# Hybrid encoder trunk: another order for the first projection of each layer's head, and thirteen idle transposes left out

## The reference

```python
h = layer_norm(x, ln_in_g, ln_in_b)
for l in range(DEPTH):                       # DEPTH = 2
    proj = h @ w_in[l]                       # 1024 x 2048
    ...                                      # four head groups: windowed attention, gated conv, Fourier mixing, rotary attention
    mix = jnp.concatenate([rms_norm(o, g_i) for each group], axis=-1)
    h = layer_norm(DN_ALPHA * h + mix @ w_out[l], ln1_g[l], ln1_b[l])
    ffn = jnp.square(jax.nn.relu(h @ w1[l])) @ w2[l]
    h = layer_norm(DN_ALPHA * h + ffn, ln2_g[l], ln2_b[l])
return h
```

## Time and profile before

| | |
|---|---|
| median of 3 runs | 1072.41 us (1072.38 to 1072.66) |
| profiled execution | 1072.76 us |
| its span, first to last instruction | 1071.1 us |
| PE busy | 1054.8 us, 98% |
| DVE, ACT, POOL busy | 788.7, 516.7, 91.6 us |
| share of PE in the chain that ended last | 91% |
| mean granted TensorE clock | 0.997 |

### The profile page before, as it was taken

How to read it: one execution, slowest core, us unless ns; L and a number is a source line. 1 busy time by engine, 2 the same in 40 slices (tenths; PEclk the granted TensorE clock), 3 DMA queues, 4 the chain that set the end, 5 groups by cost and what they waited for, 6 DMA issues and landing times.

```text
span 1071.1 us, 15587 instructions
## 1 busy us (share of the span) xinstructions
PE 1054.8 (98%) x5310; PEld 896.2 (84%) x5310; DVE 788.7 (74%) x1096; ACT 516.7 (48%) x774; POOL 91.6 (9%) x84
## 2 busy tenths in 40 slices
PE   8999999999999999999999999999999999999996
PEld 6888889998888888888878888899888888888885
DVE  8845886968757758758887568777794784784787
ACT  3433666365355355355624247653643643642651
POOL 5200232100000000000002003221000000000001
PEclk9999999999999999999999999999999999999998
DMA  7432013030521520431233410310234134125122
GB/s 288 158 118 79 1 61 119 2 126 32 205 79 40 181 93 34 166 113 50 109 136 143 157 40 21 118 41 14 114 118 158 40 114 161 39 94 181 39 79 80
DMA packets 17383, 105.54 MB, mean 99 GB/s; under 512 B 2017, under 2 KB 2705, under 8 KB 5793
## 3 DMA queue, kind: packets, MB, share of 16 engines
q1 hardware_dynamic: 15984, 98.70, 25.3%
q0 software_dynamic: 1184, 5.86, 1.7%
q10 hardware_dynamic: 144, 0.07, 0.0%
HBM read 101.49 MB, written 2.10 MB: 97 GB/s over the span
## 4 chain that ended last, share of the span: by engine, by line
PE 91%; issue 4%; DVE 3%; ACT 0%; POOL 0%; DVEq 0%; POOLq 0%
PE bank L449 18%; PE bank L451 18%; PE bank L450 18%; PE bank L753 8%; PE bank L754 8%; PE bank L755 8%; PE bank L699 4%; PE bank L685 2%; PE bank L596 1%; PE bank L597 1%; PE bank L458 1%; PE bank L609 1%; DVE w_raw L1182 0%; PE bank L521 0%; PE bank L522 0%
## 5 line engine op out<-in xcount | busy, mean ns | idle before, releaser
L449 PE MATMUL bank<-h_hi,w_hi 128*128 128x512 f32 (+1 forms) x704 | 260.8, 370 | 0.2
L450 PE MATMUL bank<-h_lo,w_hi 128*128 128x512 f32 (+1 forms) x704 | 260.3, 370 | 0.0
L451 PE MATMUL bank<-h_hi,w_lo 128*128 128x512 f32 (+1 forms) x704 | 260.3, 370 | 0.0
L753 PE MATMUL bank<-w_hi,hid_hi 128*128 128x512 f32 x448 | 174.4, 389 | 0.0
L754 PE MATMUL bank<-w_lo,hid_hi 128*128 128x512 f32 x448 | 174.3, 389 | 0.0
L755 PE MATMUL bank<-w_hi,hid_lo 128*128 128x512 f32 x448 | 174.3, 389 | 0.0
L1163 DVE TENSOR_TENSOR w_lo<-w_raw,w_hi 128x2048 fp32r<-128x2048 f32 x62 | 141.8, 2287 | 36.8 <-ACT w_hi L870 30.0
L449 PEld LDWEIGHTS bank<-h_hi,w_hi 128*128 128x128 f32 x704 | 132.6, 188 | 23.5 <-issue 1.1
L451 PEld LDWEIGHTS bank<-h_hi,w_lo 128*128 128x128 f32 x704 | 132.6, 188 | 22.6
L450 PEld LDWEIGHTS bank<-h_lo,w_hi 128*128 128x128 f32 x704 | 132.6, 188 | 22.3
L870 ACT CAST w_hi<-w_raw 128x2048 fp32r<-128x2048 f32 x56 | 107.1, 1913 | 79.5 <-PE bank L755 56.4
(11 more groups left out here) (174 smaller groups left out, 1638.5 us busy)
## 6 DMA issues: line engine op xcount, KB each, us to landing
w_raw<-in_weights SPq DMA_DIRECT2D x63, 1024.0 KB, 4.8
w_third<-in_weights SPq DMA_DIRECT2D x23, 1024.0 KB, 4.8
rows<-in_rows POOLq DMA_DIRECT2D x4, 1024.0 KB, 5.0
w_raw<-in_weights SPq DMA_DIRECT2D x4, 512.0 KB, 7.3
out_h<-x SPq DMA_DIRECT2D x8, 256.0 KB, 2.0
x<-in_x SPq DMA_DIRECT2D x3, 512.0 KB, 9.6
dft<-in_dft SPq DMA_DIRECT2D x2, 512.0 KB, 7.1
qk_gain<-in_qk_gain POOLq DMA_DIRECT2D x3, 192.0 KB, 3.6
```

Of the source, the lines that this page charges most:

```text
L449: pe.matmul(dst, s_hi, m_hi, start=first, stop=False)
L450: pe.matmul(dst, s_hi, m_lo, start=False, stop=False)
L451: return pe.matmul(dst, s_lo, m_hi, start=False, stop=last)
L753: pe.matmul(bank[dst + t][:], s_hi, m_hi, start=start, stop=False, skip_group_check=goes_on)
```

## The change

Two engines get another order, and thirteen transposes go.

PE: `keep_warm(8)` becomes `keep_warm(1)` and `keep_warm(6)` is left out. In the loop, tile 0 starts with the two products of its own high part with kt 0 and 1, which wait for h_hi only and no longer for h_lo; then the two with its low part, then the two with the low weights of kt 0 and 1; then kt 2 to 7, own high and low in pairs. The turn of tile 1 stands behind all of these. Then come low weights kt 2 and 3 of tile 0, tile 1's eight products of the own high part and its eight of the low part, low weights kt 4 to 7 of tile 0, the turn of tile 2, and the low weights of tile 1. As before, one order serves both layers.

DVE, in layer 1's head alone: the two halves of h_lo of tile 0 now stand between the two halves of tile 1's statistics, and behind its variance.

```diff
-            keep_warm(8)
+            keep_warm(1)
             turn(0, 0)
-            keep_warm(6)
             with pe.Fori(0, DEPTH) as l:
...
-                for t in range(2):
-                    for kt in range(KT):
-                        if t == 0 and kt == 4:
-                            turn(l, 1)
-                        if kt % 4 == 0:
-                            wait(pe, l, "h_lo", 2 * t + kt // 4 + 1)
-                        if t == 0:
-                            high_part_ready(l, kt // PARTS, kt % PARTS)
-                        dst, t_hi, t_lo, m_hi, _ = first_group(t, kt)
-                        pe.matmul(dst, t_hi, m_hi, start=kt == 0, stop=False)
-                        pe.matmul(dst, t_lo, m_hi, start=False, stop=False)
-                for t in range(2):
-                    for kt in range(KT):
-                        if t == 0:
-                            part_ready(l, kt // PARTS, kt % PARTS)
-                        if t == 1 and kt == 0:
-                            turn(l, 2)
-                        dst, t_hi, _, _, m_lo = first_group(t, kt)
-                        last = pe.matmul(dst, t_hi, m_lo, start=False, stop=kt == KT - 1)
-                    last.then_inc(sems["products"], 1)
+                def high_parts(t, kts, own_high):
+                    for kt in kts:
+                        if kt % 4 == 0:
+                            wait(pe, l, "h_hi" if own_high else "h_lo", 2 * t + kt // 4 + 1)
+                        if t == 0 and own_high:
+                            high_part_ready(l, kt // PARTS, kt % PARTS)
+                        dst, t_hi, t_lo, m_hi, _ = first_group(t, kt)
+                        pe.matmul(dst, t_hi if own_high else t_lo, m_hi, start=own_high and kt == 0, stop=False)
+
+                def low_parts(t, kts):
+                    for kt in kts:
+                        if t == 0:
+                            part_ready(l, kt // PARTS, kt % PARTS)
+                        dst, t_hi, _, _, m_lo = first_group(t, kt)
+                        last = pe.matmul(dst, t_hi, m_lo, start=False, stop=kt == KT - 1)
+                    if kt == KT - 1:
+                        last.then_inc(sems["products"], 1)
+
+                first_half, second_half = range(KT // 2), range(KT // 2, KT)
+                for own_high in (True, False):
+                    high_parts(0, range(2), own_high)
+                low_parts(0, range(2))
+                for kt in range(2, KT):
+                    high_parts(0, (kt,), True)
+                    high_parts(0, (kt,), False)
+                turn(l, 1)
+                low_parts(0, range(2, 4))
+                for half in (first_half, second_half):
+                    high_parts(1, half, True)
+                for half in (first_half, second_half):
+                    high_parts(1, half, False)
+                low_parts(0, second_half)
+                turn(l, 2)
+                low_parts(1, range(KT))
                 for t in range(2, TOK):
...
             first_norm(0)
-            input_stats(1)
-            stream_low(0, 0, 0)
+            dve.wait_ge(x_landed[1], 16)
+            row_stats(1, 0)
+            low_half(0, 0, 0, 0)
+            row_stats(1, 1)
+            variance(1, 4, 2, LN_EPS)
+            low_half(0, 0, 0, 1)
             first_norm(1)
```

## The result

| | before | changed |
|---|---|---|
| median, 21 runs each | 1072.85 us (1072.29 to 1074.31) | 1074.31 us (1073.74 to 1075.86) |
| profiled execution | 1072.76 us | 1075.03 us |
| its span | 1071.1 us | 1073.3 us |

The ratio is 1.0014, 95% interval 1.0008 to 1.0020: the changed kernel is slower by 0.9 to 2.1 us of 1073. Forecast were +1.6 us, ratio 1.0015, and a range that holds the measured time; the change is within the 0.2% that the prediction took for the least that can be told from no change. The profiled execution of the change, 2.27 us above that of the kernel before, is one of its slower ones.

The account below looks back on a forecast made before the run. PE's own work was taken to set the time, so order matters only where PE waits, at the two layers' heads. Layer 2 +2.62 and layer 1 -1.03 give +1.6 us, 1074.0 us on the median; range 1073.1 to 1075.1.

Parts of the forecast that it names:

- Layer 2's loss: Layer 2's head: ten more products and a wait delay tile 1's turn; DVE's list carries the whole +2.62 us on.
- the one wait for w_lo part 1: Layer 2's head: PE waits 0.24 us for DVE's part 1 and pays some 0.10 us for a start from idle.
- The further 0.1 for each other wait: Layer 2's head, upper bound +2.8 us: each semaphore wait among the first six products costs a further 0.1.
- Layer 1's start: Layer 1's head: h_hi comes earlier, so PE's first product starts at 10.12 instead of 11.82, -1.70 us.
- Layer 1's gain: Layer 1's head: tile 2's turn at 21.82 instead of 22.85, its products from 24.52 instead of 25.55, -1.03 us.
- a lead of 0.05 was enough: Layer 1's head: DVE, due 0.07 us ahead of POOL, takes the shared port first, as it did in layer 2.
- the first rival: Layer 1's head: POOL has the port before DVE; gain 0.26 instead of 1.03, total +2.36, 1074.8 us; chance 0.24.
- the precedent: Layer 2's head: DVE led POOL's rstd by 0.05 us and had its normal length, while rstd took 1.05 instead of 0.55.
- the forecast order: Layer 1's head: DVE's first centring instruction of tile 2 goes before POOL's part 6 at the shared port.
- The late clock: Layer 1's head: TensorE's clock rises later, tile 0's products run at half speed; total about +3.1, 1075.5 us; chance 0.08.
- The sum: Both heads together: +2.62 - 1.03 = +1.6 us, put on the median as 1074.0 us, +0.15%.

Follow-up runs that it names:

- turn by layer: Changed kernel with tile 1's turn behind eight products in layer 2, as before, and low weights kt 0 and 1 of tile 0 behind that place: 1071.97 us, ratio 0.9989.

## Why the prediction was right

**Layer 2's loss: right, a little small.** Forecast +2.62 us with the bounds 2.3 and 2.8; between the two places lie 528.04 instead of 525.27, +2.77. The mechanism was DVE's list, as said: only its start moved (idle 0.55 to 3.19), its length is 10.02 us as before. Most of the missing 0.15 is in the one wait for w_lo part 1: it cost 0.44 us (0.90 from 537.45 to 538.35, where two products take 0.46) and not 0.34, because DVE began its parts 0.24 us behind PE's first product (536.66 against 536.42) and not 0.14 as in the earlier trace rows. In the second trace, where they began 0.14 behind (537.08 against 536.94), the turn came 4.58 us behind the first product; the forecast makes it 4.55. The further 0.1 for each other wait, which the prediction gave as its upper bound, did not come: the starts behind the first, which takes 0.33 us as before, are 0.23 to 0.24 us apart. Moving the turn alone brings 15.78 of 15.8 forecast, and taking it back for layer 2, together with the two products with low weights, brings the old distance.

**Layer 1's start: right in the first trace.** First half of h_lo 9.91 (10.02 forecast), first product 10.02 (10.12), w_lo part 2 at 12.31 (12.40), tile 1's turn 14.52 (14.56), DVE's centring 17.74 (17.85), part 6 at 17.83 (17.92). The constant 0.1 us is the trace's earlier start of tile 0's norm.

**Layer 1's gain: the step "a lead of 0.05 was enough" failed.** The instant of arrival was forecast within 0.02 us, but the conclusion from it was not safe. In the change's own trace the first rival happened with its numbers: part 7 at 20.80 (20.88), tile 2 at 25.07 (25.19). With DVE first it is 24.30 and 24.43 (24.52). In the row that I took as the precedent, POOL had been idle for 5.28 us before its rstd; here part 6 comes right behind another instruction of its own. That this makes the difference is only argued, and with part 6 behind another instruction both orders occurred. So the chance given to the forecast order rested on a sign that does not decide.

**The late clock** did not come over the products in the change's traces, but was near: the clock rose at 10.01, 10.37, 10.00 and 8.83 us there. In the first three all eight transposes of tile 0's turn went at 1.2 GHz, 0.21 us apart, and in the second the clock was up only behind the first product (10.21). With the idle transposes left out of the kernel before it fell to 1.2 GHz over eight products. (The rises are from the clock records of the traces. The windows' granted clock reads 1.00 also ahead of the first record, where transposes 0.213 us apart show the half clock.) The Trainium skill's sentence in "TensorE: Matmul & The Clock Gate", "Part 4: PE-mode transpose", that the full clock does not engage for transposes, is not borne out by any trace here: in the three traces of the kernel before the clock rose at 7.61 to 9.74 us, with nothing but transposes run, and the transposes behind the rise went 0.11 us apart instead of 0.21.

**The sum: right in the medians, not in the traces.** Forecast were +2.62 and -1.03. In the traces layer 1's gain is only 0.2 us (tile 2 at 25.00 on the mean of four and at 25.19 on the mean of three), and the traced executions of the two kernels differ by 2.5 us on the mean (1075.0 and 1072.5), where the timed ones differ by 1.46 and 1.74. The medians of the series with the turn by layer give both terms without a trace: +2.74 for layer 2, and -1.00 for layer 1. The gain has a wide interval, 0.2 to 2.1 us (from 0.9980 to 0.9998), so it fits the forecast and does not prove it. From the first series (1.69 us around each span, 520.25 behind layer 2's tile 2, and the distances of the table) tile 2 of layer 1 would stand at 24.3 in the usual execution of the change and at 25.6 in that of the kernel before, a gain of 1.3.

So the agreement of the number is in part luck. The step on the port failed, three of four traces went the way of the first rival, and the profiled execution lies 2.27 us above that of the kernel before, which is the rival's +2.36. What brings the usual execution to a gain of about 1 us stays open. The traced execution stands 0.7 and 0.8 us above the median of its series in the two series of the change, and 0.2 to 0.75 us below it in the seven others that were timed and traced in the experiments. So it is not a shift that the profiler gives to every kernel; chance in clock, port and landings, or a shift in the change alone, would both do.

## What to carry to other kernels

Where one order of instructions is shared by the passes of a loop, reckon a move in each of them: what lies idle in the first can stand ahead of a full queue in the second. What a moved instruction costs is to be read on the engine that waits for it, not on its own, and there from the length of the list behind it to the next thing that the bounding engine needs. And an "idle" instruction should be left out only where others take its place, so that the clock is held.

## What the runs showed of the hardware

- DVE (two inputs in SBUF) and POOL (reading SBUF) alternate by whole instructions, and the one that waits comes next even if the holder's next instruction has already begun by the record: in the change's first trace DVE's ended 0.55 us after POOL's part 6, part 7 (recorded from 19.07) ended 1.15 us after DVE's first, and DVE's second 0.55 us after part 7. With one input in PSUM DVE passes freely (1.40 and 2.55 us side by side). With a recorded lead of 0.08 to 0.10 us for DVE, POOL was first in three executions and DVE in two.
- The moment at which TensorE's clock rises is not the same in executions of one kernel: 7.6 to 9.7 us in three of the kernel before, 8.8 to 10.4 in four of the change. In the kernel before, tile 2 of layer 1 came up to 0.6 us later with it.
- Between the two passes of the loop on PE, the last product of one and the first of the next start 0.23 to 0.90 us apart in the thirteen traces, 0.26 to 0.90 in the four of the change alone, and the profile shows no releaser for it.
